# Hybrid retention / gated-delta encoder block: 24 projection tiles of the second block computed beside the first block's mixing and kept in DRAM, the first adaptive pieces summed on VectorE, six MLP tiles held for the last window

## What is computed

```
mod = silu(c) @ ada_w + ada_b            # six vectors: shift, scale, gate (mixing), shift, scale, gate (MLP)
h    = rmsnorm(x) * (1 + scale_a) + shift_a
proj = h @ w_in                          # 4 retention heads and 4 gated-delta heads
mixed = [retention(proj), gated_delta(proj)]
x = x + gate_a * (mixed @ w_out)
h = rmsnorm(x) * (1 + scale_m) + shift_m
x = x + gate_m * (relu(h @ w_ff1)**2 @ w_ff2)
out = rmsnorm(x)
```

## Time and profile before

| | |
|---|---|
| median of 3 runs | 3024.84 us (3022.74 to 3027.2) |
| the profiled execution's own time | 3023.29 us |
| its span in the trace | 3021.5 us, mean granted clock 0.984 |
| PE busy | 2892.4 us, 96% |
| DVE, ACT, POOL busy | 44%, 39%, 57% |
| chain that ended last | PE 86%, DVE 5%, POOL 4% |

### The profile page before, as it was taken

One profiled execution on the slowest core, in us unless ns is written; L12 is line 12 of the kernel. 1 busy time (PEld: TensorE's weight loads), 2 busy tenths in 40 slices (PEclk: granted clock), 3 DMA queues, 4 the chain that ended last, 5 costly groups with the idle time before them and its releaser, 6 DMA issues.

```text
span 3021.5 us, 38391 instructions
## 1 busy us (share of the span) xinstructions
PE 2892.4 (96%) x14600; PEld 2425.1 (80%) x14600; DVE 1327.2 (44%) x1885; ACT 1168.0 (39%) x2032; POOL 1734.8 (57%) x1320
## 2 busy tenths in 40 slices
PE   8999879999999999999999999999999999899998
PEld 7777767878888788888888788887888888678886
DVE  2566755453435335463434435545343433421223
ACT  1343443343344434353433433444333333343332
POOL 1555554575656656575556655657565665566553
PEclk9999998999999999999999999999999999999999
DMA  6233313222232323422233323422222222423332
GB/s 237 77 112 131 135 56 105 70 88 76 86 118 84 101 70 112 133 74 86 76 111 99 91 88 92 146 74 85 80 84 78 88 81 88 143 78 97 98 98 84
DMA packets 86582, 295.12 MB, mean 98 GB/s; under 512 B 10240, under 2 KB 10240, under 8 KB 82304
## 3 DMA queue, kind: packets, MB, share of 16 engines
q1 hardware_dynamic: 64944, 247.05, 25.8%
q10 hardware_dynamic: 21456, 45.62, 4.5%
...
## 4 chain that ended last, share of the span: by engine, by line
PE 86%; DVE 5%; POOL 4%; issue 2%; ACT 2%; DMA 0%; ACTq 0%; SPq 0%; POOLq 0%; DVEq 0%
PE acc L421 23%; PE acc L423 23%; PE acc L422 23%; PE pm L456 7%; PE pm L461 3%; PE pm L586 2%; POOL w L1466 1%; POOL mT L1475 1%; DVE mixing L1071 1%; ACT io L684 1%; PE pm L437 1%; PE pm L550 1%; DVE io L987 1%; POOL hid L1480 1%; PE pm L470 0%
## 5 line engine op out<-in xcount | busy, mean ns | idle before, releaser
L1466 POOL TENSOR_TENSOR w<-raw,w 128x512 fp32r<-128x512 f32 x832 | 1119.0, 1347 | 1037.3 <-ACT w L658 990.2
L658 ACT ACTIVATE w<-raw 128x512 fp32r<-128x512 f32 x832 | 521.2, 628 | 750.3 <-PE acc L423 680.7
L421 PE MATMUL acc<-mT,w 128*128 128x512 f32 x1280 | 516.2, 403 | 13.4 <-POOL mT L1475 6.1
L423 PE MATMUL acc<-mT,w 128*128 128x512 f32 x1280 | 500.3, 391 | 0.0
L422 PE MATMUL acc<-mT,w 128*128 128x512 f32 x1280 | 499.2, 390 | 0.0
L421 PE MATMUL acc<-hT,w 128*128 128x512 f32 x1024 | 435.5, 425 | 24.6 <-POOL w L1466 10.7
L423 PE MATMUL acc<-hT,w 128*128 128x512 f32 x1024 | 406.9, 397 | 0.0
L422 PE MATMUL acc<-hT,w 128*128 128x512 f32 x1024 | 405.6, 396 | 0.0
L1282 DVE SCALAR_TENSOR_TENSOR x<-acc,ab,x 128x512 f32<-128x512 f32 x256 | 191.5, 750 | 450.4 <-PE acc L423 450.2
L421 PE MATMUL acc<-hid,w 128*128 128x512 f32 x896 | 364.5, 407 | 13.8 <-POOL hid L1480 8.3
L423 PE MATMUL acc<-hid,w 128*128 128x512 f32 x896 | 350.3, 391 | 0.0
...
## 6 DMA issues: line engine op xcount, KB each, us to landing
raw<-in_w_all SPq DMA_DIRECT2D x416, 512.0 KB, 3.6
...
xr<-in_xT ACTq DMA_DIRECT2D x48, 256.0 KB, 3.2
...
out<-io ACTq DMA_DIRECT2D x32, 256.0 KB, 2.8
mixed_kept<-mixing ACTq DMA_DIRECT2D x28, 256.0 KB, 2.0
xr<-mixed_kept ACTq DMA_DIRECT2D x28, 256.0 KB, 2.7
...
```

What stands on the lines that cost most here:

```text
L421: e.matmul(bank, whi, x[:, 0, :], start=first, stop=False)
L423: m = e.matmul(bank, wlo, x[:, 0, :], start=False, stop=last)
L658: e.activation(w2[:, 0, local % HALVES, :], raw[:, tile % NRAW, local % 2 * NT:(local % 2 + 1) * NT], ACT.Copy).then_inc(S["w_hi"], 1)
L1466: e.tensor_tensor(w2[:, 1, local % HALVES, :], raw[:, tile % NRAW, local % 2 * NT:(local % 2 + 1) * NT], w2[:, 0, local % HALVES, :].bitca ...
```

## The change

1. **Projection tiles of block 1 early.** h of block 1 is made in the prologue, into `hT`; block 0's h goes into `mT` instead. Windows 0, 1 and 2 hold 12 tiles (8 of the next unit and 4 of block 1), window 3 holds 12 of block 1, window 4 the last 8. All 32 projection tiles of block 1 are evacuated by ACT to `ffs`, stored to a DRAM tensor `proj_kept` (`keep`, `kept_store`), and read back from it by ACT's queue in windows 3 to 6 (`kept_load`, at slots 18 to 32). Windows 5 and 6 so hold 20 tiles, all MLP, and window 7 holds 24 where it held 32.
2. **First adaptive pieces on DVE.** `mod_direct` goes; `first_sum` sums the 8 pieces on DVE (128x2048 each), and 16 small matmuls follow (`mod_columns(0)`). The first norm's squares are added on POOL instead of DVE, and half of the multiplications of x by the root too. The later pieces are loaded in halves.
3. **Six MLP tiles held.** Window 15 holds 18 tiles (24 before) with another order; the last six `FF2` tiles of block 2 go into window 16: two before `OUT`, four between `OUT` and the first `FF1`. Block 3 has a residual of its own (`x1_late`), and block 2's final norm moves from window 16's first slots to its slots 41 and later.
4. The order of tiles in windows 7 and 11 changes a little, and some semaphores are merged.

```diff
         if b == 0:
-            new, per = p, [1] * SLOTS
+            if u + 1 < HEADS:
+                e = kept[4 * n:4 * n + 4]
+                new = p[0:2] + e[0:1] + p[2:5] + e[1:2] + p[5:6] + e[2:3] + p[6:7] + e[3:4] + p[7:8]
+            else:
+                new = kept[12:24]
+            per = even(KT * len(new))
         elif n == UNITS:
...
-            per = [0] * 8 + [3] * 21 + [1] + [0] * 10 + [22] * 23 + [6]
+            held = ff(b - 2, NG - 2)[1][2:4] + ff(b - 2, NG - 1)[1]
+            new = held[0:2] + new[0:KT] + held[2:6] + new[KT:]
+            per = [2] * 8 + [3] * 21 + [1] + [3] * 9 + [5] + [22] * 23 + [6]
...
+        elif b == 1 and u < HEADS - 1:
+            f = [ff(b - 1, g) for g in range(NG)]
+            if u == 1:
+                new = f[1][0] + f[1][1] + f[2][0] + f[2][1] + f[3][0]
+            else:
+                new = f[3][1] + f[4][0] + f[4][1] + f[5][0] + f[5][1]
+            per = even(KT * len(new))
+        elif b == 1:
+            (a6, c6), (a7, c7) = (ff(b - 1, g) for g in (6, 7))
+            new = (a6 + p[0:2] + c6[0:2] + p[2:3] + c6[2:4] + p[3:5] + a7 + p[5:7] + c7[0:2] + p[7:8] + c7[2:4])
...
-                new = (a5[0:3] + p[0:1] + a5[3:4] + p[1:2] + c5[0:2] + p[2:3] + c5[2:4] + a6[0:1] + a6[1:4] + p[3:4]
+                new = (a5 + p[0:2] + c5[0:2] + p[2:3] + c5[2:4] + a6 + p[3:5] + c6 + a7 + p[5:7] + c7[0:2] + p[7:8]
...
-                new = a5 + c5 + a6 + c6 + a7 + c7
-                per = [3] * SLOTS
+                new = a5 + c5 + a6 + a7 + c6[0:2]
+                per = [3, 2] * 26 + [1] * 10 + [2] * 2
```

```diff
 # SP, prologue
+            e.dma_start(x1[:, :, :], xT[0]).then_inc(S["x1_in"], 16)
+            for k in range(KT):
+                ada_load(k)
             load(0)
             load(1)
...
             e.dma_start(lmask[:, :, :], masks[:, 4:4 + LEVELS, :]).then_inc(S["lmask_in"], 16)
...
 # PE, prologue
-            for k in range(KT):
-                mod_direct(k, bC)
-                if k == 5:
-                    column_sums(0, bB)
-                if k == 6:
-                    row_everywhere(0, bA)
+            column_sums(0, bB)
+            row_everywhere(0, bA)
+            mod_columns(0, bC)
             for d in range(UNIT * KT):
                 dense(d)
...
                 if d == 2 * KT - 1:
                     gate_columns(0, bF)
+                    column_sums(NORM["h", 1], bE)
+                if d == 3 * KT - 1:
+                    row_everywhere(NORM["h", 1], bD_)
...
 # DVE, prologue
+            for k in range(KT):
+                first_sum(k)
+                if k == 4:
+                    scaled_sums(0, bB)
+                if k == 5:
+                    diagonal(0)
...
 # POOL, prologue
             e.wait_ge(S["const_in"], 32)
             e.wait_ge(S["lmask_in"], 16)
             e.wait_ge(S["host_consts"], 3)
+            for j in range(1, KT):
+                e.wait_ge(S["sq_ready"], j + 1)
+                if j > 1:
+                    e.wait_ge(S["sq_added"], j - 1)
+                e.tensor_tensor(sqrow, sqrow, io[:, j % 2, :], ALU.add).then_inc(S["sq_added"], 1)
...
 # ACT
+            def kept_load(n, i):
+                at = UNIT * (n - HEADS) + i
+                e.wait_ge(KEPTOUT[at % 2], 16 * (at // 2 + 1))
+                proj_free(n, i)
+                dst = pg[:, i, HIST:HIST + NT] if i < 3 else pr[:, i - 3, :]
+                e.dma_start(dst, proj_kept[at]).then_inc(S["kept_in"], 16)
```

More of the change, by code:

```diff
@@ L52, in proj, with even @@
         return (PROJ, n, i, 0)
+    def even(count):
+        return [(s + 1) * count // SLOTS - s * count // SLOTS for s in range(SLOTS)]
     def ff(b, g):
@@ L61, in dense_plan @@
         p = [proj(n + 1, i) for i in range(UNIT)]
+        kept = [proj(HEADS + q, i) for q in range(HEADS) for i in range(UNIT)]
         if b == 0:
-            new, per = p, [1] * SLOTS
+            if u + 1 < HEADS:
[4 more added lines that the diff above has]
+            per = even(KT * len(new))
         elif n == UNITS:
@@ L329, in hidden, with residual @@
         def hidden(b, g):
+            if b == NB - 2 and g == NG - 1:
+                return hT[:, :, 0:FFG, :]
             return hid_late if b == NB - 1 and g % 2 else hid
+        def residual(b):
+            return x1_late if b == NB - 1 else x1
         def ring_in(key):
@@ L367, in _ @@
             e.dma_start(cs[:, 1, :], sin[0]).then_inc(S["cs_in"], 16)
-            for k in range(KT, KT + 4):
-                ada_load(k)
+            for part in range(4):
+                late_load(part)
             for g in range(NRAW, len(TILES)):
                 load(g)
-                window, i = divmod(g - UNIT - 6, UNIT)
-                if 0 <= window < 3 and i < 4:
-                    e.wait_ge(S["ada_sums"], 4 * window + i + 1)
-                    ada_load(KT + 4 + 4 * window + i)
+                for part in range(4, ADA_PARTS):
+                    window, i = divmod(part - 4, len(ADA_SLOTS))
+                    if g == UNIT + PER_WINDOW * window + ADA_AFTER[i]:
+                        late_load(part)
         @block.tensor
@@ L744, in dense @@
                 if k == KT - 1 and kind == PROJ:
-                    evac(g)
+                    keep(g) if b // HEADS == 1 else evac(g)
                 if k == KT - 1 and kind == FF1:
@@ L870, in _ @@
             e.activation(wgs[:, 0, :, :], wg[:, :, :], ACT.Copy).then_inc(S["wg_split"], 1)
-            for h in range(3):
-                hi(h)
             e.wait_ge(S["x1_in"], 16)
@@ L884, in _ @@
                 evac(i)
+                for j in {0: (0, 1, 2, 3), 1: (4, 5, 6, 7)}.get(i, ()):
+                    sem, count, x = ring_in(("sq", 1, j))
+                    e.wait_ge(sem, count)
+                    square(NORM["h", 1], j, x)
+                    if j < 4:
+                        ring_load("sq", 1, j + 4)
+                    else:
+                        ring_load("xn", 1, j - 4)
                 if i == 1:
@@ L1357, in _ @@
             e.sem_inc(S["mod_ready"], 1)
+            e.wait_ge(S["x0_ready"], 4)
             e.wait_ge(S["xn_ready"], KT)
@@ L1402, in _ @@
                         mix(n, s)
-                    if u == 0 and b >= 2 and s in (8, 9):
-                        for j in (4, 5) if s == 8 else (6, 7):
+                    if u == 0 and b >= 2 and at in (8, 9):
+                        for j in (4, 5) if at == 8 else (6, 7):
                             out_tile(b - 2, j)
@@ L1438, in _ @@
                     if u == 3 and b + 1 < NB:
-                        if b == 0 and s == 0:
-                            for j in range(2, KT):
-                                next_normed(b + 1, j)
                         if b and s < 4:
@@ L1555, in _ @@
                 lo(2 * i + 4)
-                for s in {5: range(42), 6: range(42, 57), 7: range(57, SLOTS)}.get(i, ()):
+                if i == 2:
+                    rms_power(NORM["h", 1])
+                for s in {4: range(42), 5: range(42, 57), 6: range(57, SLOTS)}.get(i, ()):
                     front(0, s)
+                if i >= 5:
+                    for j in (2 * (i - 5), 2 * (i - 5) + 1):
+                        low_part(SPLIT["h", 1], hT, j)
+            for j in (6, 7):
+                low_part(SPLIT["h", 1], hT, j)
             for n in range(UNITS + 1):
@@ L1565, in _ @@
                         gdn_power(n - 1)
-                    if u == 0 and b >= 2 and s == 4:
+                    if u == 0 and b >= 2 and s == (45 if n == UNITS else 4):
                         rms_power(NORM["f", b - 2])
@@ L1583, in _ @@
                     if u == 3:
-                        if b == 0 and s == 0:
-                            for j in range(KT):
-                                low_part(SPLIT["h", b + 1], hT, j)
                         if b and b + 1 < NB and s < 4:
```

361 lines of the change are left out of this document (217 added, 144 removed).

## The result

The changed kernel took 2996.4 us (median of 4 runs, 2992.31 to 2997.52) against 3025.03 us of before (4 runs, 3022.74 to 3027.2): a ratio of 0.9904, 95% interval 0.9892 to 0.9917. It is faster, as forecast, but by 29 us and not by 68; 2996.4 lies just outside the range (2925 to 2995). The sign was right and the size wrong by more than half.

A forecast was written before the change was run, and what follows sets the result against it. PE, 96% busy, was taken as the bound, so only its idle or lower-clock time could be gained. Terms -5 + 16 - 66 + 9 + 2 - 24 = -68 gave 2957 us, range 2925 to 2995 for 8 in 10.

The forecast's parts named there:

- Term 3: Windows 0 to 3: longer slots let DVE catch up, block 1's norm and low parts leave; -66 us.
- one of its own signs: Windows 0 to 2: the prediction falls if PE waits for weights in them.
- Rival B: Windows 0 to 3: 32 added POOL low halves hold DVE 1.35 us each; 2992 us; chance 0.17.
- Term 4: MLP, windows 5 and 6: five bare `FF1` to `FF2` transitions lose about 1.9 us each; +9 us.
- Term 6: Tail, windows 15 and 16: held `FF2` tiles cover the last unit's end and block 2's norm; -24 us.
- Term 2: Prologue: block 1's norm added, 5.0 us stall behind tile 2, POOL too full in tiles 5 to 8; +16 us.
- Term 1: Start: small matmuls on raw pieces go, POOL's additions wait for level masks; first dense matmul at 66.5, -5 us.
- Term 5: Windows 7 and 11: less work above POOL's low-half chain for weights; +2 us in window 7, zero in 11.
- Rivals C: Start and prologue: norm hidden, DVE's sums end earlier; -10 instead of +11, 2936 us; chance 0.22.
- D: Windows 0 to 3: a unit's chain stretches with added tiles; 66 us stay, 3023 us, no change; chance 0.03.
- E: SP's weight loads stand behind 28 waits on DVE's adaptive sums and hold PE; slower, 3033 us; chance 0.05.

## Why the prediction was right or wrong

**Term 3 failed, by 18.4 of 37.** The step was "DVE is behind from slot 28 to 46; 18 slots give it 6.2 us more, and the wait there was 4.1, so it goes". It assumed a backlog that drains over 18 slots. The timelines of both kernels show DVE idle and waiting for PE at slot 40, then 10 to 11 us of work that arrives at once: more time per slot ahead of the burst is worth nothing, and only slots 40 to 46 (6 x 0.34 = 2.0 us by the prediction's own rate) could pay. Of them 1.2 came, 4.1 to 2.9, since the burst itself grew from 9.7 to 10.5. Moving two DVE sums (-2.8 a window) or two POOL operations (-3.9) out of the burst cured it, and windows 1 and 2 came to the 96 that was forecast. Window 3 had the same fault at slot 42 (117.0 for 112; 111.5 with the sums moved). Window 0 (102.8 for 96) has it once, and POOL's backlog from the prologue, which the ledger of the prediction ended at the window's border: `w` 3.2 at its slot 7. By one of its own signs, that PE waits for weights in these windows, the prediction fell there.

**Rival B named the cause and not the place.** Its mechanism, DVE and POOL keeping each other from SBUF, is what stretches the burst: shown by the run that moved POOL's two operations alone. But the 32 added low halves of weights, on which B's price stood, were not it; in the runs that reach 95.5 they are all still there, and all that the fuller POOL can have added to DVE's burst is 0.8 us a window (9.7 to 10.5). That 2992 came out near the result is chance. The Trainium skill, page "SBUF — State Buffer", section "Who interferes with whom", has the two excluding each other for a whole instruction; the trace agrees in the main, with 1.39 against 2.8 us for POOL's addition. What I did with the rule was to weigh it as a sum over a window, where it acts on one burst.

**Term 4 was mis-sized, 17.6 for 9.** The transitions are where they were put, but five cost 10.9 of wait, 2.2 each and up to 2.9, and not 1.9; and in window 6 the wait of block 2's norm for its diagonal grew from 0.4 to 2.0, which no term held. The clock behind each was not counted at all. The run with one tile between got 8.5 back.

**Term 6 came to -18.4 for -24.** Window 15 came as forecast (130.2 for 131); window 16 took 444.5 for 438, where PE waited five times 1.5 to 2.2 us, for the norms, for DVE's evacuations and for low parts of h. The run without the held tiles puts the holding at 19.

**Term 2, +19.9 for +16.** The wait behind tile 2 was 4.8 for 5.0, and the two waits for POOL's weights in tiles 7 and 8 came to 6.0 for 5.3. What was too small is the clock, taken at half of 5 us: two spells of 6.8 us at 0.50, with the waits of 4.8 and 4.1, cost up to 6.8, and the prologue was granted 0.91. Taking the first wait away gave 8.6 in the prologue for 4.8 of wait. **Term 1** was right: masks at 36.3, additions at 36.76, first dense matmul at 68.3 for 66.5. Of the 1.8, 0.6 are the sixth sum begun later (48.56 for 48), 0.9 the 3.07 us power, which ended that much after the sum, and 0.3 the last steps. But its bound "-25 if the masks' wait costs nothing" was too far: the run without it gave -18. **Term 5** was right in its mechanism: window 7 took 173.6 for 177 (175 in the other runs of the same order), still released by POOL's weights (4.2).

**Rivals C, D and E fall.** The prologue did not hide its norm, the tiles did fill, and no transfer held PE in windows 0 to 3. Taken by its halves, the first part of the change is the norm moved, -27 in two windows and +27 ahead of them, and the tiles moved, -28 and +19.
